# Three stages reordered, w_ada's transfers issued by ScalarE, and three output projections begun inside the attentions

## The reference, cut to what matters

```
first:  h = rmsnorm(x); proj = h @ w_in
        ya = (sigmoid(mo) * head_norm(mLSTM(silu(conv(mq, mk)), mv, mi, mf))) @ w_br_m      4 heads of 128
        yb = head_norm(softmax(q1 k1 + bias) v - lam * softmax(q2 k2 + bias) v) @ w_br_d    4 heads, causal
        x += (sigmoid(g_a) * ya + sigmoid(g_b) * yb) @ w_out
        x += (gelu(gate) * value) @ w_down        with u = conv(rmsnorm(x) @ w_up)
        x += sigmoid(rmsnorm(x) @ w_ple_gate) * (p @ w_ple);  x = rmsnorm(x)
second: x += (stick_breaking(q, k, v) * silu(gate)) @ w_out        16 heads of 64
        x += (mla(...) * silu(gate)) @ w_out                       8 heads, 128 + 64 rope
third:  mod = silu(c) @ w_ada + b_ada                              w_ada is 1024 x 9216: 36 MB
        swiglu FFN; hybrid mixer (spatial gating, and forgetting attention of 8 heads); swiglu FFN,
        each with shift, scale and gate of mod
```

## Time and profile before

| | us |
|---|---|
| median of 3 runs | 2800.07 |
| lowest, highest | 2797.7, 2801.03 |
| the profiled execution | 2803.21 |
| its span in the trace | 2801.4 |
| granted clock of TensorE over the span | 0.943 of full |

### The profile page before, as it was taken

One profiled execution on the slowest core, in us unless ns is written; L12 is line 12 of the kernel. 1 busy time (PEld: TensorE's weight loads), 2 busy tenths in 40 slices (PEclk: granted clock), 3 DMA queues, 4 the chain that ended last, 5 costly groups with the idle time before them and its releaser, 6 DMA issues.

```text
span 2801.4 us, 31055 instructions
## 1 busy us (share of the span) xinstructions
PE 2522.2 (90%) x11612; PEld 2011.9 (72%) x11612; DVE 1355.2 (48%) x1879; ACT 1018.2 (36%) x1320; POOL 1012.3 (36%) x758
## 2 busy tenths in 40 slices
PE   6889676789999889998898799999989998799996
PEld 5677555668888668776776677888858666588885
DVE  6345545586666664344434555322265433622225
ACT  4334444442122353566435533222234332321211
POOL 3223123344545344222342234454434203244442
PEclk9889888899999999999998999999989988999998
DMA  3121166523222222111122112223212101122221
GB/s 131 62 72 46 68 240 229 192 112 105 90 104 90 75 90 77 61 46 46 60 90 76 46 61 76 104 90 104 91 60 95 61 16 58 45 93 96 99 91 59
DMA packets 35813, 245.51 MB, mean 88 GB/s; under 512 B 3935, under 2 KB 3935, under 8 KB 7044
## 3 DMA queue, kind: packets, MB, share of 16 engines
q1 hardware_dynamic: 34704, 241.73, 24.0%
q10 hardware_dynamic: 1012, 2.45, 0.3%
HBM read 242.06 MB, written 2.11 MB: 87 GB/s over the span
## 4 chain that ended last, share of the span: by engine, by line
issue 58%; POOL 26%; PE 13%; DVE 2%; DVEq 1%; POOLq 0%; ACT 0%; ACTq 0%
POOL WL L290 26%; PE PS L320 4%; PE PS L321 4%; PE PS L322 4%; DVE X L2296 0%; DVE ARENA L2291 0%; DVE ARENA L1649 0%; POOLq L294 0%; DVEq L2295 0%; DVE ARENA L1667 0%; DVEq L1977 0%; DVE ARENA L1674 0%; DVEq L1690 0%; PE PS L382 0%; POOLq L287 0%
## 5 line engine op out<-in xcount | busy, mean ns | idle before, releaser
L290 POOL TENSOR_TENSOR WL<-WT,WH 128x512 fp32r<-128x512 f32 x754 | 1012.1, 1374 | 1750.4 <-ACT WH L993 1232.1
L320 PE MATMUL PS<-HH,WH 128*128 128x512 f32 x1568 | 631.2, 403 | 64.4 <-POOL WL L290 41.9
L321 PE MATMUL PS<-HL,WH 128*128 128x512 f32 x1568 | 622.3, 397 | 0.0
L322 PE MATMUL PS<-HH,WL 128*128 128x512 f32 x1568 | 621.0, 396 | 0.0
L320 PEld LDWEIGHTS PS<-HH,WH 128*128 128x128 f32 x1568 | 301.7, 192 | 146.5 <-POOL WL L290 45.7
L1310 ACT CAST WH<-WT 128x2048 fp32r<-128x2048 f32 x90 | 172.1, 1912 | 603.7 <-PE PS L320 603.7
L320 PE MATMUL PS<-YH,WH 128*128 128x512 f32 x840 | 335.9, 400 | 52.1 <-POOL WL L290 23.9
L322 PEld LDWEIGHTS PS<-HH,WL 128*128 128x128 f32 x1568 | 301.6, 192 | 65.3
L321 PEld LDWEIGHTS PS<-HL,WH 128*128 128x128 f32 x1568 | 302.0, 193 | 60.6 <-issue 0.5
L322 PE MATMUL PS<-YH,WL 128*128 128x512 f32 x840 | 331.6, 395 | 0.0
L321 PE MATMUL PS<-YL,WH 128*128 128x512 f32 x840 | 331.6, 395 | 0.0
(11 more groups left out here) (290 smaller groups left out, 3408.3 us busy)
## 6 DMA issues: line engine op xcount, KB each, us to landing
WT<-weights SPq DMA_DIRECT2D x188, 1024.0 KB, 4.8
ARENA<-w_ada SPq DMA_DIRECT2D x36, 1024.0 KB, 5.5
X<-x_fm SPq DMA_DIRECT2D x4, 512.0 KB, 8.2
out_fm<-X SPq DMA_DIRECT2D x8, 256.0 KB, 2.0
ARENA<-rel_rows ACTq DMA_DIRECT2D x1, 1024.0 KB, 5.4
CON<-constants SPq DMA_DIRECT2D x1, 704.0 KB, 9.9
WT<-weights SPq DMA_DIRECT2D x1, 512.0 KB, 5.8
ARENA<-rows SPq DMA_DIRECT2D x1, 512.0 KB, 3.9
```

The lines of the kernel that those rows point to most:

```text
L290: i = nc.gpsimd.tensor_tensor(WL[s][:, e], WT[s][:, e], WH[s][:, e].bitcast(F32), ALU.subtract)
L320: i0 = nc.tensor.matmul(o, w[0], r[0], start=first, stop=False, skip_group_check=True)
L321: nc.tensor.matmul(o, w[0], r[1], start=False, stop=False, skip_group_check=True)
L322: i2 = nc.tensor.matmul(o, w[1], r[0], start=False, stop=last, skip_group_check=True)
```

## The change

Six edits. (1) SP issues only the first three transfers of w_ada and then streams panels; ACT issues the other 33, each behind the second sum of the buffer that it overwrites. (2) mLSTM: on PE half of a head's scores move behind the next head's projection tile, and the values behind a second one; ACT and DVE follow. (3) Differential attention: DVE does the reciprocal in halves, and the finish, one head later, between the row maximum and the wait for the exp. (4) Stick-breaking: 42 of the 48 matmuls of output projection 2's first panel move ahead of the last pair's cumulative sums. (5) MLA: likewise DVE's gap is filled, ACT's cast moves behind the tile, and 42 matmuls of output projection 3 move into tiles 26 to 31. (6) Forgetting attention: 24 matmuls of output projection 4 move into tiles 24 to 31, three each, and the sum of squares goes to PSUM bank 6.

```diff
@@ SP: w_ada's transfers @@
-            def ada(aidx, s, first=False):
-                if not first:
-                    sp.wait_ge(sem("ada_used"), aidx - 2)
-                sp.dma_start(ADA[s], ...).then_inc(sem(f"ada_dma{s}"), 16)
             for k in range(3):
-                ada(k, k, first=True)
-            for i in range(12):
-                panel(G_MERGE + 2 + i, (G_MERGE + 2 + i) % 2)
-                for k in range(3 if i < 10 else 0):
-                    ada(3 + 3 * i + k, k)
-            stream(G_MERGE + 14, G_FFN1)
-            for k in range(3):
-                ada(33 + k, k)
-            stream(G_FFN1, G_FFN1 + 2)
+                sp.dma_start(ADA[k], ada_in[k]).then_inc(sem(f"ada_dma{k}"), 16)
+            stream(G_MERGE + 2, G_FFN1 + 2)
@@ ACT: ada_sums, behind the second sum of a buffer @@
                     if j % 2:
                         i.then_inc(sem("ada_used"), 1)
+                        t = j // 2 + 3
+                        if t < NADA:
+                            act.wait_ge(sem("ada_used"), j // 2 + 1)
+                            act.dma_start(ADA[t % 3], ada_in[t]).then_inc(sem(f"ada_dma{t % 3}"), 16)
@@ PE: mLSTM @@
             for h in range(M_HEADS):
-                m_score(h)
+                m_score(h, 0)
                 ...                       # m_max(h + 1), m_tile(h + 1, 1)
-                m_values(h)
+                m_score(h, 2)
                 ...                       # m_tile(h + 2, 0)
+                m_values(h)
@@ ACT: mLSTM @@
-                m_num(h)
                 if h + 2 < M_HEADS:
                     next_panel(G_MQK + h + 2)
-                    m_silu(h + 2, 0)
                 ...
+                m_num(h)
+                if h + 2 < M_HEADS:
+                    m_silu(h + 2, 0)
+            act.wait_ge(sem("rel_out"), 16)
+            act.dma_start(BT, ...).then_inc(sem("bt_dma"), 16)   # was inside the last head
@@ DVE: mLSTM @@
-                m_weights(h)
+                m_weights(h, 0)
                 if h + 1 < M_HEADS:
-                    dve.drain()
                     m_arg(h + 1)
+                m_weights(h, 2)
@@ DVE: differential attention (da_softmax split before its wait for the exp) @@
             for v in range(DA_TILES):
                 if v + 1 < DA_TILES:
                     da_softmax(v + 1)
+                    if j == 3 and h:
+                        da_recip(h - 1, 0)
+                    if j == 0 and h >= 2:
+                        da_recip(h - 2, 1)
+                    if j == 1 and h >= 2:
+                        da_finish(h - 2)
+                    if j == 2 and h + 2 < DA_HEADS:
+                        da_bias(h + 2)
+                    da_scale(v + 1)
                 if j == 0 and h:
                     da_out(h - 1)
-                if j == 3 and h:
-                    da_finish(h - 1)      # with the whole reciprocal in it
-                if j == 3 and h + 2 < DA_HEADS:
-                    da_bias(h + 2)
@@ PE: a step of an output projection @@
+            def out_step(g, src, ready, c, b, k):
+                pe.wait_ge(sem(ready), k + 1)
+                i0, i2 = exact3(psb(b), wtile(g % 2, 8, 256, k, c, c + P), (src[0][:, k, :], src[1][:, k, :]), k == 0, k == DT - 1)
+                if c == 0 and k == 0:
+                    used(g, i0)
+                if k == DT - 1:
+                    i2.then_inc(sem("a_done"), 1)
@@ PE: stick-breaking attention, last pair p @@
+                else:
+                    open_panel(G_OUT2)
+                    ob = take(), take()
+                    for e in range(2):
+                        for k in range(DT - 1):
+                            out_step(G_OUT2, (YH, YL), "sy_ready", P * e, ob[e], k)
@@ PE: MLA attention, tile v @@
+OUT3_STEPS = {26: ((0, 0), (0, 1), (0, 2)), 27: ((0, 3), (0, 4)), 28: ((1, 0), (1, 1), (1, 2)), 29: ((1, 3), (1, 4)),
+              30: ((0, 5), (1, 5)), 31: ((0, 6), (1, 6))}
+                for e, k in OUT3_STEPS.get(v, ()):
+                    ...                   # open_panel(G_OUT3) and take() where k is 0
+                    out_step(G_OUT3, (YH, YL), "mly_ready", P * e, ob[e], k)
@@ ACT: MLA attention @@
+                if j == 2 and h + 2 < MLA_HEADS:
+                    mla_proj(h + 2, "q")
                 if v + 1 < n["att"]:
                     mla_exp(v + 1)
-                if j >= 2 and h + 2 < MLA_HEADS:
-                    mla_proj(h + 2, j == 3)     # at j 2: next_panel, q, k; at j 3: rope
+                if j == 2 and h + 2 < MLA_HEADS:
+                    mla_proj(h + 2, "k")
+                if j == 3 and h + 2 < MLA_HEADS:
+                    mla_proj(h + 2, "r")
                 ...                       # copy of the transposed tile
+                if j == 3 and h + 2 < MLA_HEADS:
+                    next_panel(mlh(h + 2))
@@ DVE: MLA attention (mla_softmax split likewise) @@
                 if v + 1 < NQ * MLA_HEADS:
                     mla_softmax(v + 1)
+                    if j == 1 and h:
+                        mla_out(h - 1)
+                    if j == 2 and h + 1 < MLA_HEADS:
+                        mla_keys(h + 1)
+                    mla_scale(v + 1)
-                if j == 0 and h:
-                    mla_out(h - 1)
-                if j == 1 and h + 1 < MLA_HEADS:
-                    mla_keys(h + 1)
@@ PE: forgetting attention, tile v @@
+                if v >= FOX_TILES - 8:
+                    e, k = divmod(v - FOX_TILES + 8, 4)
+                    ...                   # open_panel(G_OUT4) and take() where k is 0
+                    out_step(G_OUT4, (YH, YL), "gy_ready", P * e, ob[e], k)
@@ PE: behind its last tile @@
-            b = take()
-            gate_sums(1, range(3), b)
+            pe.wait_ge(sem("fo_read"), 3)
+            gate_sums(1, range(3), 6)
             fox_values(FOX_TILES - 1)
-            gate_sums(1, (3,), b).then_inc(sem("a_done"), 1)
+            gate_sums(1, (3,), 6).then_inc(sem("gsum_ready"), 1)
-            ...                           # all 48 matmuls of the panel, k 0 to 3, then 4 to 7
+            for e in range(2):
+                for k in range(4, DT):
+                    out_step(G_OUT4, (YH, YL), "gy_ready", P * e, ob[e], k)
```

More of the change, by code:

```diff
@@ L478, in m_max, with m_score @@
                 nc.tensor.matmul(psb(2), pick(h, 4), LROW[2][0:4, :], start=True, stop=True).then_inc(sem("mb_ready"), 1)
-            def m_score(h):
+            def m_score(h, i0):
                 pe.wait_ge(sem("mqk_ready"), 2 * (h + 1))
-                for i in range(NQ):
+                for i in (i0, i0 + 1):
                     u = NQ * h + i
@@ L748, in _ @@
                 m.then_inc(sem("so_ready"), 1)
-            out_gemm(G_OUT2, (YH, YL), "sy_ready")
+            for e in range(2):
+                out_step(G_OUT2, (YH, YL), "sy_ready", P * e, ob[e], DT - 1)
+            for g in range(G_OUT2 + 1, G_OUT2 + 4):
+                open_panel(g)
+                feature_tiles(g, g % 2, 8, 256, y_hi, y_lo, (0, P))
             fresh_h()
@@ L839, in _ @@
             n["att"] = NQ * MLA_HEADS
+            ob = {}
             mla_score(0)
@@ L850, in _ @@
                     mla_proj(h + 2, j == 3)
+                for e, k in OUT3_STEPS.get(v, ()):
+                    if k == 0:
+                        if e == 0:
+                            open_panel(G_OUT3)
+                        ob[e] = take()
+                    out_step(G_OUT3, (YH, YL), "mly_ready", P * e, ob[e], k)
                 pe.wait_ge(sem("pn_ready"), v + 1)
@@ L859, in _ @@
             mla_values(n["att"] - 1)
-            out_gemm(G_OUT3, (YH, YL), "mly_ready")
+            for e in range(2):
+                out_step(G_OUT3, (YH, YL), "mly_ready", P * e, ob[e], DT - 1)
+            for g in range(G_OUT3 + 1, G_OUT3 + 4):
+                open_panel(g)
+                feature_tiles(g, g % 2, 8, 256, y_hi, y_lo, (0, P))
             ffn(G_FFN2, shift=0)
@@ L1470, in mla_v, with mla_proj @@
                         free(nc.scalar.copy(LV[:, t, S * c:S * (c + 1)], psb(b)), b)
[L1472 to L1477, removed]
+            def mla_proj(h, kinds="qkr"):
                 for k, g in ((0, "qn_g"), (2, "kn_g")):
+                    if "qk"[k // 2] not in kinds:
+                        continue
                     b = take()
@@ L1481, in mla_proj @@
                     free(f(QKT[h % 2][:, k, :], psb(b), ACT.Copy, scale=par(g)), b)
+                if "r" in kinds:
+                    b = take()
+                    f(SQR[:, 1, :], psb(b), ACT.Square).then_inc(sem("hsq_ready"), 1)
             def mla_root(h):
@@ L1509, in _ @@
                 h, j = divmod(v, NQ)
+                if j == 2 and h + 2 < MLA_HEADS:
+                    mla_proj(h + 2, "q")
+                if j == 1 and h + 1 < MLA_HEADS:
+                    skip(1)
                 if v + 1 < n["att"]:
@@ L1584, in gate_root @@
             def gate_root(q):
-                b = take()
```

(11 more changed lines are left out.)

40 lines of the change are left out of this document (28 added, 12 removed).

## The result

The changed kernel takes 2670.28 us (median of 4 runs, 2669.37 to 2670.85) against 2799.09 (2797.7 to 2801.03): a ratio of 0.9538, 95% interval 0.9524 to 0.9552. That is 128.8 us less, where 104 were forecast.

The account below looks back on a forecast made before the run. PE was taken as the bound, busy 2522 of 2801 us, with its idle and lower-clock time to win. Terms -60 - 19 - 7 - 8 - 17 - 3 + 10 = -104 took 2803.2 to 2699, median 2696; range 2660 to 2742.

Parts of the forecast that it names:

- Transfers of w_ada: Merge stage: ACT issuing the transfers lets weight panels go a panel ahead; passes of 37 us, -60 (-27 to -75).
- The ring: Merge stage, three w_ada buffers: three rounds priced at 30 us; as rival, late landings, passes of 47, 2729, chance 0.16.
- mLSTM: Moved scores and values give DVE time; period 23.62 to 17.3 at full clock, three periods: -19 (-8 to -24).
- Differential attention: DVE's moved reciprocal saves about one reciprocal for each of two heads: -7 (0 to -11).
- Stick-breaking: 42 matmuls fill PE's 9.95 us wait for LBH; next panel then starts after its WL: -8 (-5 to -9.5).
- MLA: Without PE's wait for ACT's copy of q behind the cast, period 17.4 for 20.3, six heads: -17 (-8 to -25).
- the early steps: Output projection 3's first-panel 42 matmuls go into MLA tiles with gaps; memset and accumulator read bound the second: -3 (-6 to +3).
- Forgetting attention: Last eight tiles: 24 added matmuls cost 10.8 us at clock 0.50, and nothing comes back behind the last tile: +10.
- I take the half clock: Forgetting attention: three matmuls per tile, about half of what tiles with panels had, leave the clock at 0.50.
- The rival that the clock rises: Forgetting attention: dense steps among the tiles raise the clock, -7 for +10, 2679; chance 0.25.
- ACT's in-order queue as a loss: Merge stage: ACT waits for each w_ada landing; at 17 us passes take 72, whole kernel slower, 2807; chance 0.03.
- the attentions with unchanged periods: mLSTM, differential attention, MLA: a chain over three engines keeps the periods; -14 in place of -46, 2728; chance 0.14.

Follow-up runs that it names:

- ada_coupled: Kernel before with ACT issuing 33 w_ada transfers, but SP still waiting for ACT's sums before each merge-stage weight panel: 2794.23 us, ratio 0.9992.
- ada_only: Kernel before with only the w_ada edit: ACT issues 33 of the transfers, SP streams panels: 2730.21 us against 2797.97, ratio 0.9764.
- after_nofox: Changed kernel with the forgetting-attention edit undone (no output projection 4 matmuls in tiles 24 to 31): 2675.75 us, ratio 0.9566 to the kernel before.
- mla_cast: Changed kernel with ACT's weight-panel cast back ahead of the copy of q in tile 2 of each MLA head: 2670.58 us.
- fox_only: Kernel before with only the forgetting-attention edit (24 matmuls into tiles 24 to 31, sum of squares in bank 6): 2797.78 us, ratio 0.9984.
- acc_spread: Changed kernel with DVE's memset ahead of output projection 3's read-out cut into eight pieces: 2680.46 us, ratio 0.9587 to the kernel before.
- no_out3: Changed kernel with output projection 3 whole behind the MLA attention again, without early matmuls in the tiles: 2670.07 us.

## Why the prediction was right, and where it was wrong

The forecast was 26 us too long. In the profile 22.7 us come from the forgetting attention, the one stage that moved the other way. The other stages come within 5 us of their sum, and that is in part luck: mLSTM, differential attention and the merge stage gave 14.5 us more than forecast, stick-breaking and MLA 9.4 less.

**Transfers of w_ada: right.** -67 for -60, and -63 to -67 by the spread of the kernel before. The queue order was the cause (ada_coupled). Of the four resources PE (33 us), the DMA share and ACT came out about as worked out, and the passes at 34.7 to 36.5 for 37. The ring did not: the landing rose from 5.2 to 7.3 us, and three rounds are 3 x (7.3 + 4.85) = 36.5 in place of 30, as long as the pass. VectorE waits 27.2 us for landings in the three passes and ACT 15.5 for VectorE, which is the sign that the prediction had named for the ring; but the casts aren't late by it, and the price of 47 a pass didn't come. Whether the ring, the DMA engines or PE now sets the pass no run separates. An issue leaves ACT idle for 0.41 us, the issue of 0.33 within it, where 0.6 was taken. The Trainium skill's sentence on issuing engines (DMA: Bandwidth & Descriptors, Issuing engines are not separate DMA queues) agrees with the runs: a second issuer alone left the median as it was in ada_coupled (ratio 0.9992), and with the order freed the DMA share is 0.92 to 0.96.

**mLSTM: right in kind, short in size.** -25.2 for -19. The period is 16.62 at clock 1.00, all of it PE; I had 17.3, which is 2 us over three periods. The term also left out the interval from cast 7 to 8, which shrank more than a period (22.39 to 13.51), and whose cast now also stands earlier in ACT's order. Another 1.3 us are not the change's: cast 6 to 7 took 18.94 us in the profile of before (clock 0.89), but 17.58 in ada_only, with the same code.

**Differential attention: -8.3 for -7.** The size fits; no run took it alone, so that the moved reciprocal is the cause is argued, not shown.

**Stick-breaking: -5.1 for -8.** The 42 matmuls did fill the wait (9.95 us, now 0.38), at full clock. What came late next was not the WL of the next panel, as the term had it, but the last YL, with a wait of 3.9 us, which is of the size of the missing 3. POOL's subtraction now runs beside VectorE's split, and the cast of 0.43 us takes 1.38, the subtraction of 0.69 takes 1.59. No run took this part alone.

**MLA: the wrong step and the wrong sign of a term.** -13.5 for -20, and -10 to -13.5 by the spread of the kernel before. The period came out at 17.7 for the 17.4 forecast, but not by the step that I named: with the cast ahead of q's copy again the head is 0.7 us shorter, not 1.8 longer. The earlier trace rows names the copy as the last to come; that doesn't say that the cast ahead of it is what makes it late. For the early steps I took -3; they cost 3.8 in the stage and 6.7 where they stand. About half of that is the memset (3 us), which I had seen, the other half the hole behind the attention, which I hadn't.

**Forgetting attention: wrong, and the largest miss.** +10 forecast, -12.7 in the profile. The step that failed is "I take the half clock". The rival that the clock rises had the mechanism at -7 (2679 in all); measured, the stage is 12.7 shorter than before, and 6.7 shorter than after_nofox, where the clock holds throughout. What neither had is that the same code in this stretch gives two outcomes, and that without part 6 too the clock doesn't always fall at the same place. The rule that I set against the row, of the Trainium skill (TensorE: Matmul & The Clock Gate, Part 1: The HAM clock gate), that activity releases the throttle, agrees only in part. PE was busy for 94% of the stretch before, at a mean clock of 0.76, and for 88% of it in the changed kernel, at 0.95. The slower matmuls themselves make the first share larger, so the busy share alone doesn't tell here which clock is granted. Where the clock had fallen it came back either with the 128x512 steps among the tiles, or behind the last tile, during the 128x512 matmuls of the sum of squares.

Some readings of the prediction were off without moving the sum. The transfers of the earlier trace rows stop or nearly stop about three times per pass, not five or six times per 50 us. MLA's outer bound, 20.3 to 15.2 over six heads, is -31 and not -25. A 128x512 matmul at the lower level starts 0.43 us behind the one before it (1249.98, 1250.40 and 1250.83 in the changed kernel), where 0.452 was taken.

The ring as priced, ACT's in-order queue as a loss and the attentions with unchanged periods are out: passes of 35 us, heads of 16.6 and 17.7. The slower side was never near.

## What to carry to other kernels

A transfer that waits for its buffer holds up every transfer behind it in its queue (here 250.3 to 180.2 us of one stage): look for a DMA queue that waits on one stream and carries another, and let the engine that frees the buffer issue the refill. Price an idle gap twice, once for itself and once for the clock of what comes after it, and ask of work moved into a gap what it had been covering where it stood. When variants differ by less than a few us, compare a stage between two fixed points in several profiles and not the total, whose single runs lay up to 20 us apart for one and the same kernel (2788 to 2808 for the kernel before).

## What was not expected of the hardware

- Adding 48 matmuls made mLSTM 6 us shorter, by the clock (0.86 to 0.98).
- The granted clock of one piece of code is not fixed: with the same code in the last tiles of the forgetting attention it held in the changed kernel (twice) and mla_cast, and was half for 20.5 us in fox_only, acc_spread and no_out3; 9.2 us apart.
- VectorE slows beside GpSimd: in the changed kernel the 128x512 cast of the split took 1.36 to 1.39 us in the three cases beside POOL's subtraction and 0.43 in the 25 others; the subtraction behind it took 1.59 in two of the three and 0.69 where POOL was idle.
